# Hybrid RWKV-7 and attention layer on one core: the attentions moved ahead of RWKV, the queries' multipliers applied at the scores

## The reference, cut to what matters

```
h = rms(x); proj = h @ w_in            # RWKV 1792 | q 512 | k 128 | v 128 | qm 512 | gates 3072 columns
o_a = rwkv(...)                        # token shift, lora products, scan of 64-token chunks, group norm of 8 heads, * g
q = rms(q) * qn; k = rms(k) * kn       # per head of 64
o_b = softmax([q k^T / 8 - alibi, sink]) v            # windows of 128 + own chunk of 64; cache for the sample
qm = rms(qm) * mqn
o_m = softmax(qm mk^T / sqrt(128)) mv                 # 4 heads of 128, 256 memory tokens; mk = rms(..) * kn
x = x + sum_n(sigmoid(gate_n) * (o_n @ w_branch_n)) @ w_out
x = x + (gelu(conv3(rms(x) @ w_up_a)) * (rms(x) @ w_up_u)) @ w_down
```

## Time and profile before

| | us |
|---|---|
| median of 3 runs (lowest, highest) | 2242.31 (2236.42, 2245.64) |
| profiled execution, whole | 2257.36 |
| its span, first to last instruction | 2255.5 |
| mix blocks of groups 0, 1, 2 | 379.8, 392.6, 350.6 |
| TensorE busy | 2110.6 |

### The profile page before, as it was taken

The page is one execution under the profiler, slowest core; times in us unless marked ns, Lnnn a source line. Parts: engine busy times, 40 slices in busy tenths (PEclk is TensorE's granted clock), DMA queues, the critical chain, the costliest instruction groups (busy, mean ns, idle before and its releaser), DMA issues. The chain is left out here.

```text
span 2255.5 us, 40381 instructions
## 1 busy us (share of the span) xinstructions
PE 2110.6 (94%) x15682; PEld 1958.1 (87%) x15682; DVE 1200.2 (53%) x2184; ACT 954.1 (42%) x1939; POOL 1133.5 (50%) x916
## 2 busy tenths in 40 slices
PE   5979999899999998899999999999989989899998
PEld 4868888799999987788788999999878877799998
DVE  6685545355664237553554466632675355457740
ACT  5423345445444432333463444443423355355542
POOL 5533333365666654333334656665634333567776
PEclk9999999999999999999999999999989999999999
DMA  5421223463445432112225534453321232644453
GB/s 176 145 62 58 64 87 98 138 196 115 126 128 159 146 106 87 48 46 76 91 82 184 167 114 128 127 160 122 122 67 53 86 116 86 202 150 148 147 158 124
DMA packets 158141, 264.71 MB, mean 117 GB/s; under 512 B 20096, under 2 KB 53120, under 8 KB 157952
## 3 DMA queue, kind: packets, MB, share of 16 engines
q1 hardware_dynamic: 157376, 261.08, 36.7%
q10 hardware_dynamic: 576, 1.05, 0.1%
HBM read 242.60 MB, written 19.46 MB: 116 GB/s over the span
## 5 line engine op out<-in xcount | busy, mean ns | idle before, releaser
L215 POOL TENSOR_TENSOR k_w_lo<-k_raw,k_w_hi 128x512 fp32r<-128x512 f32 x832 | 1086.4, 1317 | 1028.5 <-ACT k_w_hi L206 984.6
L206 ACT ACTIVATE k_w_hi<-k_raw 128x512 fp32r<-128x512 f32 x832 | 500.1, 617 | 384.8 <-PE k_acc L237 126.4
L235 PE MATMUL k_acc<-k_x_hi,k_w_hi 128*128 128x384 f32 (+1 forms) x1152 | 422.1, 366 | 13.5 <-PEq L70 10.0
L237 PE MATMUL k_acc<-k_x_hi,k_w_lo 128*128 128x384 f32 (+1 forms) x1152 | 383.7, 333 | 0.0
L236 PE MATMUL k_acc<-k_x_lo,k_w_hi 128*128 128x384 f32 (+1 forms) x1152 | 383.6, 333 | 0.0
L235 PEld LDWEIGHTS k_acc<-k_x_hi,k_w_hi 128*128 128x128 f32 x1152 | 222.9, 193 | 52.2 <-issue 27.3
L236 PEld LDWEIGHTS k_acc<-k_x_lo,k_w_hi 128*128 128x128 f32 x1152 | 223.5, 194 | 5.7 <-issue 1.4
L237 PEld LDWEIGHTS k_acc<-k_x_hi,k_w_lo 128*128 128x128 f32 x1152 | 222.7, 193 | 0.0
L235 PE MATMUL k_acc<-g1f_xg_hi,k_w_hi 128*128 128x384 f32 x352 | 118.7, 337 | 2.2 <-DVE g1fu_a_raw L2043 2.2
L235 PE MATMUL k_acc<-g0f_xg_hi,k_w_hi 128*128 128x384 f32 x352 | 118.7, 337 | 2.2 <-DVE g0fu_a_raw L2043 2.2
L235 PE MATMUL k_acc<-k_o_hi,k_w_hi 128*128 128x384 f32 (+1 forms) x288 | 99.0, 344 | 22.2 <-POOL k_w_lo L215 10.2
(11 more groups left out here) (720 smaller groups left out, 4435.8 us busy)
## 6 DMA issues: line engine op xcount, KB each, us to landing
k_raw<-w_up SPq DMA_DIRECT2D x264, 256.0 KB, 2.6
k_raw<-w_gate SPq DMA_DIRECT2D x144, 256.0 KB, 3.1
k_raw<-w_down SPq DMA_DIRECT2D x96, 256.0 KB, 3.8
k_raw<-w_rwkv SPq DMA_DIRECT2D x84, 256.0 KB, 2.9
k_raw<-w_branch SPq DMA_DIRECT2D x72, 256.0 KB, 3.5
k_raw<-w_attn SPq DMA_DIRECT2D x60, 256.0 KB, 2.6
k_raw<-w_out SPq DMA_DIRECT2D x48, 256.0 KB, 2.9
k_raw<-w_down_end SPq DMA_DIRECT2D x24, 256.0 KB, 3.4
```

The source lines that it names most:

```text
L206: act.activation(c.w_hi[s][:, 0:n], c.raw[s][:, 0:n], ACT.Copy).then_inc(c.hi_done, 1)
L215: pool.tensor_tensor(c.w_lo[s][:, 0:n], c.raw[s][:, 0:n], c.w_hi[s][:, 0:n].bitcast(F32), ALU.subtract).then_inc(c.lo_done, 1)
L235: pe.matmul(out, wh, xh, start=(u.begins and k == 0), stop=False)
L237: mm = pe.matmul(out, wl, xh, start=False, stop=(u.ends and k == u.kt - 1))
```

## The change

1. Order of the work in a mix block: the pa units come first, then pr, then gates. The chain is attentions' prep, attentions, prep, scan, post. No chain step lies beside pa but the keys' and the first; the others are spread evenly over the last 150 half units, 1.33 a step (1.38 in the last group).
2. Attentions' prep (6 steps): ScalarE squares each pa tile in the dense thread. One matmul with `ones_head` sums the key tile, already spread. The queries' sums go to 32 partitions for each tile: eight matmuls with a 32-column left side, four into one bank, four into another. They are copied out, transposed to tokens along partitions (two transposes an item), and rooted as [128, 3, 12]. Only the keys are multiplied by gain and root; `kq` is the keys times the queries' gain.
3. Scores use the raw queries and `kq`; the bias takes each head's root from `qf` as a scalar (four operations of 256 columns instead of two of 512). Memory scores use the memory keys times the queries' gain (once in group 0, once for the sample's cache); the exponential's scale is `qf`.
4. The attentions' outputs stay in `pa`; their high and low halves are made in post, by two ScalarE and two VectorE operations of 1536 columns. `o_hi` and `o_lo` hold window, RWKV, memory.
5. DMAs: `to_rows` and `from_rows` are loaded with 4 of 9 matrices; SP issues sinks and alibi before masks and identities; the memory cache comes at the first chain step. The wait for the stores of the feed-forward block before moves from POOL to ScalarE and VectorE.

```diff
-        order = [0, 0, 1, ...] if g == 0 else [0] * 8
-        for m in range(2, R_TILES):
-            order += [0] * 4 + [1]
...
-        order += spread(2 * len(us) - 4 * R_TILES - 4, rest)
+        n_pa = 4 * A_TILES + 2
+        order = [0, 0, 1] * n_keys + [0] * (n_pa - 2 * n_keys)
+        order += spread(2 * len(us) - n_pa, N_ATTN_PREP + n_attn + N_PREP + n_scan + N_POST)
...
             def attn_prep():                                     # TensorE
-                        pe.matmul(bank[5][:, 0:T], c.to_rows[:, n, :], asq[:, n % 4, 0:T], ...)   # n of 9
-                    pe.matmul(bank[n % 5][:, 0:T], c.from_rows[:, n, :], ay[:, 0:T], ...)         # n of 9
+                pe.wait_ge(S["a_squared"], 9)
+                pe.matmul(bank[5][:, 0:T], c.ones_head[:, :], asq[:, 4, 0:T], start=True, stop=True).then_inc(S["a_rows"], 1)
+                for j in range(4):
+                    rows = slice(32 * j, 32 * j + 32)
+                    pe.matmul(bank[4][rows, 0:T], c.ones_head[:, 0:P:4], asq[:, j, 0:T], start=True, stop=True)
+                for j in range(4):
+                    rows = slice(32 * j, 32 * j + 32)
+                    mm = pe.matmul(bank[0][rows, 0:T], c.ones[:, 0:32], asq[:, 5 + j, 0:T], start=True, stop=True)
+                mm.then_inc(S["q_rows"], 1)
...
+                for n, b in enumerate((4, 0)):
+                    for p, it in enumerate(items):
+                        mm = pe.transpose(bank[b][0:it.nq, p * P:(p + 1) * P], q_rows[:, n, it.q0:it.q0 + it.nq], c.ident[:, :])
...
             def m_scores(p):                                     # TensorE
-                    pe.wait_ge(S["swa_lo"], p)
-                    pe.wait_ge(S["mem_lo"], p)
+                    pe.wait_ge(S["swa_out"], p)
+                    pe.wait_ge(S["mem_out"], p)
...
             def bias(p, half):                                   # VectorE
+                            s[p % 2][0:it.nq, i, 0:nk], bank[2 * half + e][0:it.nq, jj * 256:jj * 256 + nk],
+                            qf[0:it.nq, p, col:col + 1], c.alibi[0:it.nq, i, it.first:2 * P], ALU.mult, ALU.add)
...
             def attn():                                          # VectorE
-                    dve.wait_ge(S["mem_hi"], p + 1)
-                    dve.tensor_tensor(o_lo[:, 8:12, q], heads4[5][:, :, 0:it.nq], ...)
+                    dve.wait_ge(S["m_pv"], p + 1)
+                    dve.tensor_copy(pa[:, 5:9, q], heads4[5][:, :, 0:it.nq]).then_inc(S["mem_out"], 1)
...
             def post():                                          # VectorE
+                dve.wait_ge(S["a_hi"], 1)                        # before the root's Newton steps
+                dve.tensor_tensor(o_lo[:, O_SWA, 0:T], pa[:, 0:4, 0:T], o_hi[:, O_SWA, 0:T].bitcast(F32), ALU.subtract)
...
+                dve.wait_ge(S["a_hi"], 2)                        # behind ln_b
+                dve.tensor_tensor(o_lo[:, O_MEM, 0:T], pa[:, 5:9, 0:T], o_hi[:, O_MEM, 0:T].bitcast(F32), ALU.subtract)
...
             def chain():
-                yield from prep()
-                yield from scan()
-                yield from post()
                 yield from attn_prep()
                 yield from attn()
+                yield from prep()
+                yield from scan()
+                yield from post()
```

More of the change, by code:

```diff
@@ L157, in dense_units @@
     for g in range(len(GROUPS)):
-        for stage, w, n in (("pr", a["w_rwkv"], R_TILES), ("pa", a["w_attn"], A_TILES), ("gate", a["w_gate"], 3 * DT)):
+        for stage, w, n in (("pa", a["w_attn"], A_TILES), ("pr", a["w_rwkv"], R_TILES), ("gate", a["w_gate"], 3 * DT)):
             for m in range(n):
@@ L532 @@
 O_AT = 8 * TILE
+O_PLACE = (1, 0, 2)
+O_RWKV, O_SWA, O_MEM = (slice(4 * n, 4 * n + 4) for n in O_PLACE)
 def o_tensors(c, tag):
@@ L591, in mix_block @@
         room = place("room", [P, ROOM])
+        mask, half, one_ka = place("mask", [P, TW]), place("half", [P, 8]), place("one_ka", [P, 4])
         if g == 0:
-            early = Place(c, "g0k", place.next, c.arena_size)
+            early = Place(c, "g0k", 0, 32 * TILE)
             kxs, kt, ky = (early(n, [P, 4, MEM]) for n in ("kxs", "kt", "ky"))
@@ L616, in mix_block @@
         t1, t2, t3, sq = (give(4, TW) for _ in range(4))
-        mask, xs, t, y = (give(TW) for _ in range(4))
-        half, one_ka = give(8), give(4)
+        xs, t, y = (give(TW) for _ in range(3))
         give = rooms(0)
@@ L880, in attn_prep @@
             def attn_prep():
[L881 to L887, removed]
+                pe.wait_ge(S["a_squared"], 9)
[7 more added lines that the diff above has]
+                mm.then_inc(S["q_rows"], 1)
                 yield
                 yield
[L890 to L898, removed]
+                pe.wait_ge(S["q_read"], 1)
+                for n, b in enumerate((4, 0)):
+                    for p, it in enumerate(items):
+                        mm = pe.transpose(bank[b][0:it.nq, p * P:(p + 1) * P], q_rows[:, n, it.q0:it.q0 + it.nq], c.ident[:, :])
+                mm.then_inc(S["q_turned"], 1)
+                yield
+                yield
+                yield
+                yield
             def scores(p, half):
@@ L914, in m_scores @@
                 keys = c.mk if it.own else cmk
+                if g == 0 and p == 0 or not it.own:
+                    pe.wait_ge(S["gained"], 1)
                 if p >= 1:
-                    pe.wait_ge(S["swa_lo"], p)
-                    pe.wait_ge(S["mem_lo"], p)
+                    pe.wait_ge(S["swa_out"], p)
+                    pe.wait_ge(S["mem_out"], p)
                 for h in range(4):
@@ L1152, in attn @@
             def attn():
+                act.wait_ge(S["a_done"], 1)
+                if g > 0:
+                    act.wait_ge(S["before"], 2 if g == LAST else 1)
+                if g == LAST:
+                    act.wait_ge(S["cache"], 64)
+                k_all = slice(blocks.start * P, blocks.stop * P)
+                act.activation(kq[:, k_all], kw[:, k_all], ACT.Identity, scale=vec(c, "qn")).then_inc(S["kq"], 1)
                 act.wait_ge(S["v_turned"], 1)
@@ L1219, in dense @@
                     if ended is not None:
-                        gate_tanh(ended)
-                    ended = u if u.stage == "gate" and u.ends else None
+                        if ended.stage == "gate":
+                            gate_tanh(ended)
+                        elif ended.stage == "pa" and ended.m != 5:
+                            square(ended)
+                    ended = u if u.ends else None
                     yield
@@ L1224, in dense, with square @@
                 gate_tanh(ended)
+            def square(u):
+                n = u.m - (u.m > 5)
+                act.wait_ge(c.acc_read, u.tile + 1)
+                act.activation(asq[:, n, 0:T], pa[:, n, 0:T], ACT.Square).then_inc(S["a_squared"], 1)
             def gate_tanh(u):
@@ L1682, in chain @@
                             yield
-                for _ in range(N_POST + N_ATTN_PREP + n_attn):
+                for _ in range(N_POST):
                     yield
```

221 lines of the change are left out of this document (116 added, 105 removed).

## The result

The changed kernel takes 2266.11 us (median of 4, 2263.03 to 2271.23) where the kernel before takes 2243.97 (median of 4, 2236.42 to 2246.72): ratio 1.0098, 95% interval 1.0074 to 1.0122. It is slower by 22 us, twice what a measurement tells from no change; 2241 was forecast, with a range up to 2263.

The account below looks back on a forecast made before the run. TensorE, in order and 94% busy, was taken as the bound; other work costs only by making it wait. Terms of -23.0 - 18.8 + 1.5 + 8.6 + 16.3 + 2 + 7.6 + 4 = -1.8 us gave 2241, range 2221 to 2263.

Parts of the forecast that it names:

- part 1: Attentions' prep: fewer matmul records for row sums and spreading save TensorE time, -23.0 us (ends -25 and -13).
- part 2: Waits on root, squares, memory heads and accumulator reads go, -18.8 us; new waits in the attentions' prep, +1.5.
- part 3: RWKV's prep: 1.33 half units a step instead of four expose VectorE's chain, +8.6 us (ends 0 and +20).
- part 4: Mix block's tail: ending with the norm of heads delays the next weights, +16.3 us (+10 to +24); sliding-window low half, +2.
- part 5: Attentions: pr tiles instead of gates delay the scaling in one item a group, +7.6 us (0 to +14).
- clock: Granted clock drops behind longer waits at RWKV's kk row sums and in the tail, +4 us (0 to +8).
- rival (a): Slower: VectorE's chains at both ends of RWKV, prep and tail, are exposed in full, 2262 us; chance 0.26.
- my lower bound: Row sums' 32-partition matmuls: four records lie fully beside each other, so the 16 take 1.3 us a group.
- rival (c): Row sums: the 32-partition matmuls don't overlap, +9.6 us, 2250 us; chance 0.08.

Follow-up runs that it names:

- the second profile of the kernel before: The kernel before, unchanged, run and profiled again: 2245.44 us, ratio 0.9989; its profiled execution took 2246.56 us.
- without mixes: The changed kernel with RWKV's token-shift mixes left out, a tile's evacuation writing their place: 2242.79 us, ratio 0.9972 to the kernel before.
- mixes' work at the gates: The part-alone kernel with unused VectorE work as long as a mix after eleven gate tiles a group beside the attentions: 2258.59 us, ratio 1.0069.
- the weights behind the last step: The changed kernel with four half units of weights behind the last step of the norm of heads: 2262.47 us, ratio 1.0083 to the kernel before.
- the part-alone kernel: The kernel before with only the new row sums and the queries' multipliers at the scores, order of work unmoved: 2237.11 us, ratio 0.9951.

## Why the prediction was wrong, step by step

Measured against the second profile of the kernel before (spans 2244.7 and 2264.1 us, +19.4):

```
term                                             predicted   measured
part 1: row sums, TensorE's time                   -23.0      -21.4
part 2: waits gone / new in attentions' prep    -18.8 +1.5    -15.7 / 0
        (weights' waits, foreseen to go)                        +1.4
part 3: prep of RWKV up to the first Gram           +8.6       +1.4
part 4: block change, norm of heads              +16.3 +2      +13.1
part 5: attentions beside pr                        +7.6      +30.7
scan behind the first Gram                           0         +4.3
clock: TensorE's other work                         +4        +11.3
ffn blocks                                           0         -5.6
sum                                                 -1.8      +19.5
```

**The step that failed is part 5**, "elsewhere the tile falls outside". I had put a pr tile between score and scaling for one item a group and priced it at +3; pr tiles delay the chain of every item: the three waits of group 1 were 2.0, 0.1 and 0.1 us and are 5.8, 4.1 and 2.2. I looked only at the four half units from the memory score to the transposes, but VectorE's chain begins at the first score, six steps and eight half units ahead of the transposes in the first item. Two tiles end in that stretch, and a third is still being mixed at its start. The term also put at nothing what the tiles and the scaling lose beside GpSimd, though part 4 had seen it in ln_b: six slow scalings alone lengthen these waits by 6.1 us. The mechanism named there was the right one, as the runs without mixes and with mixes' work at the gates show; its size was 23 us too small (+30.7 for +7.6), nearly the whole error of 25 us (2241 against 2266); the other errors, -7 in part 3, -5 in part 4 and +7 in the clock among them, about cancel. That the end result is near rival (a)'s time, 2262, is luck: that rival laid it on the prep and the tail, and both came out cheaper than its upper ends.

**Part 1 held.** The row sums take 8.0 us of TensorE in three groups where they took 29.4, each record counted up to the next one's start. The open price, matmuls into 32 partitions, lay near my lower bound:

```profile
868.79 0.81 PE L890 MATMUL g1m_bank<-g1m_room,k_ones_head 128*128 128x384 f32 x2
869.53 0.88 PE L894 MATMUL g1m_bank<-g1m_room,k_ones_head 128*32 128x384 f32 x8
870.23 0.83 PE L897 MATMUL g1m_bank<-g1m_room,k_ones 128*32 128x384 f32 x8
```

Sixteen records in 1.5 us from first start to last end (869.53 to 871.06), where I took 2.0. By the Trainium skill (TensorE: Matmul & The Clock Gate, Part 3) four outputs in distinct strips take about the length of one; the trace agrees, and rival (c) is out.

**Part 2 held** but for the weights' waits: 3.5 us before, 4.8 after, at other tiles.

**Part 3 was too dark.** The wait at the row sums of kk came as foreseen (5.5 said, 4.6 measured, 2.8 before), and so did the first Gram's (4.4 said, 4.8 measured). But the spreading, said to wait 6 us as before, waits 1.0 and 1.2 where 4.4 were, since VectorE has neither pr tiles nor mixes left there: the work that hurt the attentions was taken from here. That this is the cause was not tested by itself. The wait inside the scan, put at nothing, grew by 4.3 us, and no run tells why.

**Part 4.** The branch weights wait 6.0, 6.0 and 4.6 us where 2.2, 2.1 and 2.0 were, +10.3 for +16.3: I had 14.2 us from the spreading to the next weights, and it takes 12.0 in group 1:

```profile
1204.91 2.85 PE L882 MATMUL g1m_bank<-g1m_room,k_from_rows 128*128 128x384 f32 x8 [1.75 <-DVE g1m_room L291]
...
1208.32 2.20 DVE L1472 SCALAR_TENSOR_TENSOR g1m_o<-g1m_o,k_vecs,g1m_ar 128x384 f32<-128x384 f32 x4
...
1216.90 0.66 PE L235 MATMUL k_acc<-k_o_hi,k_w_hi 128*128 128x384 f32 x1 [6.01 <-PEq L70]
```

ln_b (L1472) took 2.20 us, without the slow instance of the earlier trace rows that I had half allowed for (GpSimd's last subtraction ended at 1207.7), and the weights began 0.5 us behind VectorE's last step (1216.40), where I had 0.95.

**Clock.** TensorE's other work took 11 us longer. The mean granted clock of the whole span is 0.965 after and 0.975 before, that of the attention windows above 0.93 and 0.98, and TensorE is busy 79.7 us there for the same records that took 76.9. Chance alone does not make this: four executions of the changed kernel had 0.965 to 0.968, and 48 of the kernel before, all within 1% of its median, had 0.969 to 0.981. But it does not follow the sum of the waits either: with the weights behind the last step the sum is 11 us lower and the clock 0.962 to 0.965. What lowers it stays open.

**Against the median.** The forecast started from a profiled execution 13 us above the median and carried that difference over in full. The sum is a difference, so this moves no term. The row sums' 23.0 for 21.4 has another reason: their price, 0.322 us a record, was read at a granted clock of 1.00 and is the same in the second profile. But the next work follows the last record of each of their five bursts after 0.03 us, so that 36 records took 10.3 us and not 11.6, and the new ones 8.0 us in three groups and not 9.9.

## What to carry to other kernels

When a chain that alternates engines is moved beside other work, list what each of its engines gets between the chain's steps from the chain's very first instruction on, not from the last wait seen: TensorE's cover was the same 1.3 half units a step here, but each tile of it took 1.9 us of VectorE for 0.56, and up to 2 us more where it ran beside GpSimd. Then take off what falls into time in which that engine waits anyway, as one tile here did beside the exponentials. A change that bundles a saving with a move should be timed in parts: the saving alone was worth 11 us, 30 with its own new waits taken away, and the move cost 33. Cover for a tail only counts if no other engine's steps are ordered behind the covering work.

## What the runs showed of the hardware

Scaling (L1577, 1024 columns) takes 1.22 us on its own (0.69 at 512 columns) and up to 2.29: of 18 instances in the changed kernel six took 1.75 to 2.29, of those in the kernel before and in the part-alone kernel none took over 1.23. The order of the starts tells them apart. All six began while a GpSimd subtraction of weights was running. Six others also overlap one, for 0.5 to 1.1 us, but began before it; they take their own time, and the subtraction takes 1.7 to 2.2 us instead of 1.3. The remaining six overlap none. In the timelines above, the subtraction at 897.96 starts 0.12 us behind the first scaling and takes 2.22 us; the second scaling, from 898.98, takes 2.29.

The same holds for short instructions: the mix's first column, 128x1, takes 0.15 us, and 1.27 at 881.94, beside a subtraction. All 32 slow VectorE instructions in the attentions of the changed kernel, and all 26 with mixes' work at the gates, began while a subtraction was running. The Trainium skill (SBUF: State Buffer, Who interferes with whom) has a VectorE operation with two SBUF inputs contend with a GpSimd operation that reads SBUF, the order of issue deciding which of them waits; the trace agrees in all twelve scalings that overlap one.
